# Tile 0's norm set before the memory's, routing weights stored four to a transfer, and the first head picked from the first block of scores

## The chip, the cores and the metric

One core of one Trainium2 chip runs the whole step in one launch. The metric is the device time in microseconds (us), the median of several runs. A core has five engines, each of which runs its own list of instructions in order: TensorE (PE, matrix products), VectorE (DVE), ScalarE (ACT), GpSimd (POOL) and SyncE (SP). Here SyncE issues all direct DMAs (loads, stores, spills), and GpSimd issues the gathers of experts.

## The reference, cut to what matters

One layer is computed for 1024 prompt tokens and 64 sample tokens. The mixer has three branches that share one input projection:

```
h = RMSNorm(x)                                  # gain g_attn
cols, gates = split(h @ w_in)
x = x + (sum_b sigmoid(gate_b) * (branch_b(cols) @ w_branch[b])) @ w_out
# branches: gated linear attention, forgetting attention, attention into 256 memory tokens
mem_k, mem_v = split(RMSNorm(mem) @ w_kv)       # mem_k gets a norm of its own, per head
```

The feed-forward part retrieves single-neuron experts:

```
h = RMSNorm(x)                                  # gain g_ffn
s[t, head, side, key] = (h @ w_q) . sub_keys    # 8 heads, 2 sides, 128 keys
top 16 of each side, top 16 of the 256 sums, softmax g
y = x + sum over heads and the 16: g * gelu(u[idx] . h) * v[idx]
```

All numbers are float32. Keys and values of both attentions, the forget gates and the linear attention's state are outputs too.

## The kernel before, in words

**Tiles and groups.** Tokens are cut into tiles of 128; tiles 0 to 7 are the prompt and tile 8 is the sample (64 tokens). Tiles go in groups: tile 0 alone, 1 and 2, 3 to 5, 6 to 8. For each group there are *front* steps (everything up to the scores), and for each tile, head and pair of experts an *expert* step ("pair").

**Front steps of a group** (`front_steps`, L141): `in_prep` norms a tile's tokens and transposes them (L1174, L1394, L826); `in_unit` multiplies one of 8 column chunks of `w_in` (1.8 MB each) with a tile (L839) and spills the result to `proj` (L560); `mix` and `fox` are the three branches for a tile, from columns loaded back (`load_P`, L574); `gate` (24 products), `out` (output projection, residual, second norm), and `sco`, four blocks of 512 score columns, that is two heads each, spilled to `sc_sp` (L719, L1094).

**Weights.** SyncE loads the weights of in, gate, out and sco steps as a sequence of items into two buffers in turn (`load_item`, L501): an item is issued when the item two before has been used. `next_item` (L528) is called ahead of the store of the same step. The score weights are not an input: `sub_keys` and `w_q` are multiplied once.

**The prologue** (`pre`, 23 steps e = 0 to 22, beside the front steps of tile 0). Step 0 loads and norms the memory (SyncE L752, ScalarE L1329, VectorE L1712, which wait for ten loads on one semaphore); steps 1 and 2 transpose it, 3 and 4 multiply it with `w_kv` (32 matmuls each), 5 transposes the keys. Steps 6 to 21 are the 16 routing products (L1141): block r of `w_q` (a wq buffer, one of three, loaded by `load_wq`) times block r of the sub-keys, into the PSUM tile `p_y`. ScalarE copies the even results (L1354) and VectorE the odd (L1740) to `rw[0]` and `rw[1]`; each waits for the store two before, because it writes the buffer that this store reads. SyncE stores each block to `rw_sp` (L783) in pieces of 512 bytes. TensorE waits at each step for the copy of the one before, as `p_y` is one tile.

**Experts.** `load_sc` (L727) loads a head's 256 scores; for the first head of a group it waits until all scores of the group are stored. `pick` finds the 16 best and their weights on VectorE in four pieces (L1699), the last of which lets GpSimd gather. A pair is two gathered rows of 8 KB per token: `gather` (L1768, three pairs ahead, ring of eight buffers), `dot` (L1663), `weigh` on ScalarE (L1311), product of the diagonal weights with the values on TensorE (L1151). For tiles of the first three groups VectorE takes the value of the second expert (`values`, L1675).

**The order** is written in a plan (`make_plan`, L157): a list of entries, each with one expert (or prologue) step and the front steps beside it. All 61 front steps of tile 0 come first, 23 of them with a prologue step, then `start` (pick of the first head, first gathers), then the 64 pairs of tile 0 with the front steps of tiles 1 and 2 beside them, spread by estimated weights over the first 48, and so on. Of an entry, SyncE and TensorE run the front steps first (`walk` with `front_first`), ScalarE and VectorE the expert step first (`trail`, L468); beside a pair these two also put off the copies of in, gate and sco steps until after the next pair's step. `in_prep` of a later group waits on SyncE until all scores of the group before are stored (L544), because tokens and scores share space.

```
    plan = [(None, [s]) for s, _ in front_steps(0)]
    for e in range(PRE_STEPS):
        at = e if e < 8 else e + 2
        plan[at] = (("pre", e), plan[at][1])
    plan.append((("start",), []))
```

## Time and profile before

| | us |
|---|---|
| median of three runs | 4381.66 |
| lowest and highest | 4379.17, 4395.21 |
| the profiled execution's own time | 4382.4 |
| its span, first to last instruction | 4380.7 |

| engine | busy us | share of the span |
|---|---|---|
| TensorE, matmul | 3387.2 | 77% |
| VectorE | 2805.3 | 64% |
| TensorE, weight load | 1760.2 | 40% |
| ScalarE | 1581.6 | 36% |
| GpSimd | 1218.1 | 28% |

The mean granted clock of TensorE is 0.881 of full speed. The DMA engines move 1471.58 MB, 336 GB/s over the span; the gathers take 65.7% of their time and the direct DMAs 20.5%. The chain that ended last is TensorE for 41%, DMA for 25%, VectorE for 18%.

How to read it: times are us unless marked ns. "c_ring" is the ring of gathered experts, which the prologue uses as its working space; "c_area" holds everything of the front steps; names with _sp are spills in HBM. In the rows below, "x16" counts instructions, and "[2.49 <-DMA rw_sp<-c_ring]" is the idle time of the engine before an instruction and what ended it, as inferred by the profile. In the chain of waits each row is what the next one waited for. A DMA's row in the chain runs from its issue to its landing. PEclk is the clock granted to TensorE, as a share of full speed.

### The profile page before, as it was taken

The page shows a single profiled execution, that of the slowest core. Times are in us where ns is not written, and L with a number is a line of the kernel's source. Part 1 is how long each engine was busy: PE and PEld are TensorE (multiplying, and loading weights), DVE is VectorE, ACT ScalarE, POOL GpSimd, SP SyncE. Part 2 cuts the span into 40 slices and gives each one's busy share as a digit, 9 for nine tenths or more (in the row PEclk, how much of TensorE's full clock was granted, in tenths as well). Part 3 has the DMA queues.
Part 4 walks back from the last instruction along what each step waited for, and adds up shares of the span by engine and source line. Part 5 has one row for each costly group of instructions (what it writes and reads, how often), then busy time and mean ns, then how long its engine had stood idle before and what let it go on. Part 6 is the DMA issues. An engine that isn't in the chain of part 4 may idle for free.

```text
span 4380.7 us, 33898 instructions
## 1 busy us (share of the span) xinstructions
PE 3387.2 (77%) x10219; PEld 1760.2 (40%) x10219; DVE 2805.3 (64%) x6049; ACT 1581.6 (36%) x3679; POOL 1218.1 (28%) x1122
## 2 busy tenths in 40 slices
PE   5785867985987778989599678567978777777766
PEld 2572445842434445544144344224533222222221
DVE  0213365557657785646877788676867777667687
ACT  1212154422226563432222465344433233333333
POOL 0001111213222222323333232242323344444433
PEclk9897978997997789999799778768999889999999
DMA  4767856889986787879999798888989999999998
GB/s 174 266 236 277 327 188 235 318 335 400 346 336 228 275 305 305 344 295 371 405 394 418 299 338 299 287 333 344 414 340 382 395 415 421 414 421 413 404 371 370
DMA packets 277901, 1471.58 MB, mean 336 GB/s; under 512 B 40581, under 2 KB 91781, under 8 KB 127125
## 3 DMA queue, kind: packets, MB, share of 16 engines
q0 software_dynamic: 156672, 1140.92, 65.7%
q1 hardware_dynamic: 121044, 328.49, 20.5%
q8 instruction: 81, 1.33, 0.1%
q14 instruction: 104, 0.84, 0.1%
HBM read 1408.90 MB, written 60.40 MB: 335 GB/s over the span
## 4 chain that ended last, share of the span: by engine, by line
PE 41%; DMA 25%; DVE 18%; issue 7%; ACT 6%; POOL 2%; SPq 1%; POOLq 0%; DVEq 0%; ACTq 0%
DMA c_ring<-in_uv,l_idx 17%; PE c_p_y L1154 11%; DVE c_ring L1670 7%; PE c_PB L850 4%; PE c_PC L850 4%; DVE l_ysb L1686 3%; PE c_PA L1107 3%; PE c_PA L1062 2%; PE c_PB L1062 2%; PE c_PC L1062 2%; PE c_PB L1107 2%; POOL c_ring L1784 2%; PE c_PA L1090 1%; PE c_PC L1065 1%; PE c_PB L1065 1%
## 5 line engine op out<-in xcount | busy, mean ns | idle before, releaser
L1784 POOL DMA_INDIRECT c_ring<-in_uv,l_idx x1088 | 1211.2, 1113 | 3139.1 <-PE c_p_y L1154 1341.4
L1154 PE MATMUL c_p_y<-c_ring,l_diag 128*128 128x512 f32 (+1 forms) x2816 | 1515.6, 678 | 443.3 <-ACT l_diag L1325 433.0
L1670 DVE CUSTOM_DVE_ANT_0 c_ring<-c_ring,l_h_cur 128x1024 f32<-128x1024 f32 x1088 | 1302.8, 1221 | 369.3 <-DMA c_ring<-in_uv,l_idx 360.7
L1154 PEld LDWEIGHTS c_p_y<-c_ring,l_diag 128*128 128x128 f32 (+1 forms) x2816 | 552.9, 207 | 1233.0 <-ACT l_diag L1325 643.6
L1317 ACT ACTIVATE l_gel<-l_dots 128x2 f32<-128x2 f32 x544 | 110.7, 203 | 1607.2 <-DVE l_dots L1670 1606.0
L1686 DVE SCALAR_TENSOR_TENSOR l_ysb<-c_ring,l_wgt,l_ysb 128x1024 f32<-128x1024 f32 x384 | 492.5, 1282 | 0.0
L1317 ACT ACT_TABLE_LOAD x207 | 265.6, 1283 | 59.8 <-DVE l_dots L1670 56.5
L1320 ACT ACTIVATE l_wgt<-l_gel,l_gw 128x1 f32<-128x1 f32 x1088 | 261.2, 287 | 17.9
L1325 ACT ACTIVATE l_diag<-c_ident,l_wgt 128x128 f32<-128x128 f32 x640 | 243.0, 399 | 16.7
L850 PE MATMUL c_PB<-c_area 128*128 128x451 f32 (+1 forms) x576 | 226.3, 545 | 0.0
L850 PE MATMUL c_PC<-c_area 128*128 128x451 f32 (+1 forms) x576 | 224.4, 541 | 0.1
L1062 PE MATMUL c_PA<-c_area 128*128 128x128 f32 (+3 forms) x512 | 132.3, 415 | 70.9 <-DMA c_area<-hT_sp 47.3
L850 PEld LDWEIGHTS c_PB<-c_area 128*128 128x128 f32 (+1 forms) x576 | 106.5, 186 | 117.4 <-issue 117.4
L850 PEld LDWEIGHTS c_PC<-c_area 128*128 128x128 f32 (+1 forms) x576 | 105.2, 183 | 117.4 <-issue 116.5
L1062 PEld LDWEIGHTS c_PA<-c_area 128*128 128x128 f32 x512 | 93.4, 203 | 110.6 <-issue 81.4
L1002 PE MATMUL c_PC<-c_ident,c_area 128*128 128x128 f32 (+2 forms) x328 | 66.3, 318 | 85.4 <-ACT c_area L1261 44.5
L1107 PE MATMUL c_PA<-c_area 128*128 128x512 f32 (+1 forms) x288 | 128.9, 601 | 1.9 <-ACT c_area L1283 1.9
L1107 PE MATMUL c_PB<-c_area 128*128 128x512 f32 (+1 forms) x288 | 127.9, 597 | 1.5 <-DMA c_area<-rw_sp 1.5
L1062 PE MATMUL c_PB<-c_area 128*128 128x128 f32 (+3 forms) x512 | 123.5, 395 | 0.0
L1062 PE MATMUL c_PC<-c_area 128*128 128x128 f32 (+3 forms) x512 | 122.9, 393 | 0.0
L1570 DVE TENSOR_TENSOR c_area<-c_area,c_PA 128x128 f32<-128x128 f32 (+3 forms) x32 | 14.0, 438 | 159.1 <-ACT c_area L1274 159.1
L1090 PE MATMUL c_PA<-c_area 128*128 128x512 f32 (+1 forms) x192 | 91.9, 636 | 21.2 <-DMA c_area<-in_w_out 18.1
(275 smaller groups left out, 3676.9 us busy)
## 6 DMA issues: line engine op xcount, KB each, us to landing
c_area<-in_w_gb SPq DMA_DIRECT2D x32, 2304.0 KB, 9.5
c_area<-in_w_in SPq DMA_DIRECT2D x32, 1804.0 KB, 9.4
c_area<-rw_sp SPq DMA_DIRECT2D x16, 2048.0 KB, 10.5
c_ring<-in_uv,l_idx POOLq DMA_INDIRECT x1088, 10.1
c_area<-in_w_out SPq DMA_DIRECT2D x8, 2048.0 KB, 9.7
proj<-c_area SPq DMA_DIRECT2D x64, 225.5 KB, 7.2
c_area<-proj SPq DMA_DIRECT2D x8, 1288.0 KB, 6.6
c_area<-in_x_all SPq DMA_DIRECT2D x16, 512.0 KB, 18.8
```

Source lines behind the costliest of these rows:

```text
L850: ins = mm_(banks[2 + u % 4][:T, :PW], hT_in[:, dt, j * 128:j * 128 + T], w[:, dt * PW:(dt + 1) * PW], start=dt == 0, stop=dt == DT - 1)
L1062: mm_(ps[:, 0:N], w[:, at:at + 128], g_hT[:, e, 0:N], start=e == 0, stop=e == DT - 1)
L1065: ins = mm_(ps[:, 512:512 + N], w[:, at:at + 128], g_oT[:, 4 * b + e, 0:N], start=e == 0, stop=e == 3)
L1090: ins = mm_((PA, PB)[j % 2][:T, half * 512:(half + 1) * 512], mixT[:, dt, j * 128:j * 128 + T], w[:, dt * 512:(dt + 1) * 512], start=dt == ...
L1107: ins = mm_(banks[v % 4][:T, :], hT_out[:, dt, j * 128:j * 128 + T], w[:, dt * 512:(dt + 1) * 512], start=dt == 0, stop=dt == DT - 1)
L1154: ins = mm_(p_y[:T, e * 512:(e + 1) * 512], diag[:, j, :T], ring[:, j, D + e * 512:D + (e + 1) * 512], start=r == 0 and q == 0 and k == 0, ...
L1317: a_(gel[:, c0:c0 + PAIR], dots[:, c0:c0 + PAIR], ACT.Gelu).then_inc(s_ae, 1)
L1320: ins = nc.scalar.mul(wgt[:, c0 + k:c0 + k + 1], gel[:, c0 + k:c0 + k + 1], gw[:, head % 3, c0 + k:c0 + k + 1])
L1325: ins = nc.scalar.mul(diag[:, (n * PAIR + k) % RING, :T], unit[:, :T], wgt[:, c0 + k:c0 + k + 1])
L1670: ins = nc.vector.tensor_tensor_reduce(out=ring[:, j, 0:D], in0=ring[:, j, 0:D], in1=h_cur[i % 2][:, :], scale=1.0, scalar=0.0, op0=ALU.mu ...
L1686: nc.vector.scalar_tensor_tensor(out=y[:T, :], in0=ring[:T, j, D:2 * D], scalar=wgt[:T, col:col + 1], in1=y[:T, :], op0=ALU.mult, op1=ALU. ...
L1784: nc.gpsimd.indirect_dma_start(out=ring[:, j, :], out_offset=None, in_=t_in["uv"][:, :], in_offset=bass.IndirectOffsetOnAxis(ap=idx[:, hea ...
```

## The change

There are three parts.

1. *The plan of the prologue.* Steps 0 to 7 move two entries down: the memory's norm stands beside unit 0 of tile 0, behind its norm, and its transposes beside units 1 and 2. Units 6 and 7, which stood alone, have steps 6 and 7 beside them. The loads of step 0 are a function of their own, `pre_loads`, which SyncE calls at the end of tile 0's first `in_prep`, at the same place in its list as before.
2. *Routing weights.* `rw` becomes two buffers of four blocks each. The copies go to a quarter of one (`rw_place`); only blocks 8 and later wait for a store. SyncE stores four blocks at a time, 2 MB in pieces of 16 KB a partition, at steps 10, 14, 18 and 22. The wq buffers lie elsewhere in the ring.
3. *Scores.* The last three `sco` steps of tile 0 leave the front. They stand first in the list beside tile 0's pairs: block 1 beside the first pair, blocks 2 and 3 beside the second; the two `in_prep` loads and norms of tiles 1 and 2 stand beside the third pair instead of the first. The later steps shift by up to two pairs: attention of tile 1 starts beside pair 13 instead of 11 (counted from 0), the first gate step stands beside pair 25 instead of 24, and from `out` steps on the two plans agree within a pair. `load_sc` waits for the store of its own block alone.

```diff
@@ -157,14 +157,15 @@
 def make_plan():
 
 
-    plan = [(None, [s]) for s, _ in front_steps(0)]
+    front = front_steps(0)
+    first, rest = front[:-3], front[-3:]
+    plan = [(None, [s]) for s, _ in first]
     for e in range(PRE_STEPS):
-        at = e if e < 8 else e + 2
-        plan[at] = (("pre", e), plan[at][1])
+        plan[e + 2] = (("pre", e), plan[e + 2][1])
     plan.append((("start",), []))
     for g in range(len(GROUPS)):
         pairs = [("pair", i, r, q) for i in GROUPS[g] for r in range(HEADS) for q in range(pairs_of(i))]
-        ahead = front_steps(g + 1) if g + 1 < len(GROUPS) else []
+        ahead = (rest if g == 0 else []) + (front_steps(g + 1) if g + 1 < len(GROUPS) else [])
         total = sum(w for _, w in ahead)
         slots = len(pairs) - 2 * pairs_of(GROUPS[g][-1])
         done, k = 0.0, 0
@@ -366,8 +367,11 @@
     m_ksq = rcube(2048, MT, BW)
     m_w = [rcube(8192 + n * 4096, DT, 512) for n in range(2)]
     skT = rcube(8192, 16, NK)
-    wq = [rflat[:, 10240 + k * 1024:11264 + k * 1024] for k in range(3)]
-    rw = [rcube(13312 + k * 1024, DT, NK) for k in range(2)]
+    wq = [rflat[:, at:at + 1024] for at in (14336, 15360, 5120)]
+    rw = [rcube(at, DT, 4 * NK) for at in (1024, 10240)]
+
+    def rw_place(r):
+        return rw[r // 4 % 2][:, :, r % 4 * NK:(r % 4 + 1) * NK]
     m_gk = sb("m_gk", [128, MD])
     m_st = sb("m_st", [128, MT, 4])
     kst = sb("kst", [128, MT, 3 * MH])
@@ -512,7 +516,7 @@
             elif kind == "sco":
                 if g == 0 and n == 0:
                     for r in range(2):
-                        sp.wait_ge(s_rw[r], 16 * HEADS)
+                        sp.wait_ge(s_rw[r], 32)
                 sp.dma_start(w[:, 0:4096], rw_sp[n]).then_inc(s_w[k % 2], 16)
             else:
                 sp.dma_start(w[:, 0:4096].rearrange("p (a b) -> p a b", a=DT),
@@ -536,6 +540,18 @@
 
         def load_x(t):
             sp.dma_start(xt[t % 2][:width_of(t), :], t_in["x_all"][rows(t), :]).then_inc(s_x[t % 2], 16)
+
+        def pre_loads():
+            sp.dma_start(m_x[:, :, :], t_in["mem"].rearrange("(a p) d -> p a d", p=128)).then_inc(s_pre, 16)
+            for n in range(2):
+                sp.dma_start(m_w[n][:, :, :], t_in["w_kv"][:, n * 512:(n + 1) * 512].rearrange(
+                    "(a p) n -> p a n", p=128)).then_inc(s_pkv, 16)
+            for dst, src, n in ((m_g[:, :], t_in["mem_g_in"], D), (m_gk[:, :], t_in["mem_g_k"], MD),
+                                (wa2[:, :], t_in["gla_w_a2"][0], None), (ba_bc[:, :], t_in["gla_b_a"], 256),
+                                (go_bc[:, :], t_in["gla_g_out"], GDV), (bf_bc[:, :], t_in["fox_b_f"], FH),
+                                (gq_bc[:, :], t_in["fox_g_q"], FD), (gk_bc[:, :], t_in["fox_g_k"], FD),
+                                (gm_bc[:, :], t_in["mem_g_q"], MD)):
+                sp.dma_start(dst, src if n is None else src[0:1, :].broadcast_to([128, n])).then_inc(s_pre, 16)
 
         def in_prep(g, p):
             t0, n = first_of(g), len(GROUPS[g])
@@ -549,6 +565,8 @@
                 if n > 1:
                     load_x(t0 + 1)
                 open_run(("in", g, 0))
+                if g == 0:
+                    pre_loads()
             elif p + 1 < n:
                 sp.wait_ge(s_h, t0 + p)
                 load_x(t0 + p + 1)
@@ -727,8 +745,8 @@
         def load_sc(n):
             i, r = ALL_HEADS[n]
             g = next(g for g in range(len(GROUPS)) if i in GROUPS[g])
-            if r == 0 and i == first_of(g):
-                scores_stored(g)
+            v = sco_unit(g, r // 2, i - first_of(g))
+            sp.wait_ge(s_cput[v % 3], 16 * (v // 3 + 1))
             sp.dma_start(sc[n % 2][:width_of(i), :], sc_sp[rows(i), r * 256:(r + 1) * 256]).then_inc(s_sc[n % 2], 16)
 
         def load_h(i):
@@ -750,17 +768,6 @@
             sp.dma_start(wq[r % 3][:, :], t_in["w_qT"][r * 128:(r + 1) * 128, :]).then_inc(s_wq[r % 3], 16)
 
         def pre(e):
-            if e == 0:
-                sp.dma_start(m_x[:, :, :], t_in["mem"].rearrange("(a p) d -> p a d", p=128)).then_inc(s_pre, 16)
-                for n in range(2):
-                    sp.dma_start(m_w[n][:, :, :], t_in["w_kv"][:, n * 512:(n + 1) * 512].rearrange(
-                        "(a p) n -> p a n", p=128)).then_inc(s_pkv, 16)
-                for dst, src, n in ((m_g[:, :], t_in["mem_g_in"], D), (m_gk[:, :], t_in["mem_g_k"], MD),
-                                    (wa2[:, :], t_in["gla_w_a2"][0], None), (ba_bc[:, :], t_in["gla_b_a"], 256),
-                                    (go_bc[:, :], t_in["gla_g_out"], GDV), (bf_bc[:, :], t_in["fox_b_f"], FH),
-                                    (gq_bc[:, :], t_in["fox_g_q"], FD), (gk_bc[:, :], t_in["fox_g_k"], FD),
-                                    (gm_bc[:, :], t_in["mem_g_q"], MD)):
-                    sp.dma_start(dst, src if n is None else src[0:1, :].broadcast_to([128, n])).then_inc(s_pre, 16)
             if e == 5:
                 sp.wait_ge(s_pp, 4)
                 sp.dma_start(skT[:, :, :], t_in["sub_kT"].rearrange("h c k -> c h k")).then_inc(s_psk, 16)
@@ -778,10 +785,10 @@
                 if r + 2 < 16:
                     sp.wait_ge(s_pp, e - 1)
                     load_wq(r + 2)
-                sp.wait_ge(s_pe, e - 1)
-                dst = rw_sp[(r - 1) // 4].rearrange("p (a b) -> p a b", a=DT)
-                sp.dma_start(dst[:, :, ((r - 1) % 4) * 128:((r - 1) % 4 + 1) * 128], rw[(r - 1) % 2][:, :, :])\
-                    .then_inc(s_rw[(r - 1) % 2], 16)
+                if r % 4 == 0:
+                    sp.wait_ge(s_pe, e - 1)
+                    n = r // 4 - 1
+                    sp.dma_start(rw_sp[n], rw[n % 2][:, :, :].rearrange("p a b -> p (a b)")).then_inc(s_rw[n % 2], 16)
 
         def start():
             load_sc(0)
@@ -1353,9 +1360,9 @@
             r = e - PRE_MEM - 1
             if r >= 0 and r % 2 == 0:
                 act.wait_ge(s_pp, e - 1)
-                if r >= 2:
-                    act.wait_ge(s_rw[0], 16 * (r // 2))
-                nc.scalar.copy(rw[0][:, :, :], h3(p_y[:, :], DT)).then_inc(s_pe, 1)
+                if r >= 8:
+                    act.wait_ge(s_rw[r // 4 % 2], 16)
+                nc.scalar.copy(rw_place(r), h3(p_y[:, :], DT)).then_inc(s_pe, 1)
 
         def start():
             soften(0)
@@ -1739,9 +1746,9 @@
             r = e - PRE_MEM - 1
             if r >= 0 and r % 2:
                 dve.wait_ge(s_pp, e - 1)
-                if r >= 2:
-                    dve.wait_ge(s_rw[1], 16 * (r // 2))
-                nc.vector.tensor_copy(rw[1][:, :, :], h3(p_y[:, :], DT)).then_inc(s_pe, 1)
+                if r >= 8:
+                    dve.wait_ge(s_rw[r // 4 % 2], 16)
+                nc.vector.tensor_copy(rw_place(r), h3(p_y[:, :], DT)).then_inc(s_pe, 1)
 
         def start():
             for piece in range(4):
```

## Rows read from the trace of the kernel before

**Rows 1.** Busy by stretch: length, PE, PEld, DVE, ACT, POOL, PEclk, DMA share, GB/s

```profile
408.20:416.50 8.30, 7.08 (x20) 4.68 (x21) 8.16 (x18) 4.05 (x7) 0.00 (x0) 0.50 0.76 311
416.50:542.00 125.50, 114.47 (x297) 55.91 (x295) 50.79 (x104) 21.11 (x57) 25.00 (x22) 0.98 0.87 327
542.00:726.00 184.00, 114.26 (x514) 80.15 (x514) 113.47 (x252) 100.11 (x199) 26.77 (x26) 0.74 0.58 209
726.00:880.00 154.00, 153.61 (x640) 123.00 (x641) 78.94 (x158) 62.02 (x113) 30.50 (x28) 0.98 0.77 291
```

**Rows 2.** Chain of waits, 20 to 60 us (start us, us, what)

```profile
31.09 8.81 DMA c_gm_bc<-in_mem_g_q
...
42.27 1.28 ACT L1337
...
44.16 1.28 DVE c_ring L1718
...
50.62 1.34 PE c_p_y L1118 x8
51.96 6.15 PE c_PB L850 x16
```

**Rows 3.** DMAs issued in 8 to 9.5 us (KB each, us to landing)

```profile
c_area<-in_x_all SPq DMA_DIRECT2D x1, 512.0 KB, 3.5
c_area<-in_g_attn SPq DMA_DIRECT2D x1, 512.0 KB, 5.2
```

**Rows 4.** Chain of waits, 98 to 160 us

```profile
104.70 0.64 DVE c_area L1416
...
106.76 10.62 DMA c_ring<-in_w_qT
...
117.52 3.76 PE c_p_y L1141 x16
121.28 7.07 PE c_PB L850 x16
...
143.35 1.95 DMA proj<-c_area
```

**Rows 5.** Timeline of TensorE, 78 to 260 us

```profile
152.80 0.38 PE L868 MATMUL c_PC<-c_ident,c_area 128*16 128x128 f32 x1 [6.24 <-DMA l_V<-proj]
...
195.60 3.78 PE L1141 MATMUL c_p_y<-c_ring 128*128 128x128 f32 x16 [3.65 <-DVE c_ring L1744]
```

**Rows 6.** Timeline of VectorE, 142 to 235 us

```profile
158.80 1.23 DVE L1744 COPY c_ring<-c_p_y 128x1024 f32<-128x1024 f32 x1 [2.49 <-DMA rw_sp<-c_ring]
```

**Rows 7.** Timeline of ScalarE, 142 to 235 us

```profile
206.23 1.01 ACT L1358 COPY c_ring<-c_p_y 128x1024 f32<-128x1024 f32 x1 [9.66 <-DMA rw_sp<-c_ring]
...
221.40 1.01 ACT L1358 COPY c_ring<-c_p_y 128x1024 f32<-128x1024 f32 x1 [1.51 <-DMA rw_sp<-c_ring]
```

**Rows 8.** DMA issued at 194.8 us (KB each, us to landing)

```profile
c_ring<-in_w_qT SPq DMA_DIRECT2D x1, 512.0 KB, 9.8
```

**Rows 9.** Chain of waits, 314 to 420 us

```profile
338.61 15.46 PE c_PA L1107 x32
...
362.74 7.15 PE c_PB L1107 x16
...
370.62 7.88 DMA sc_sp<-c_area
378.52 2.30 DMA l_sc<-sc_sp
...
390.71 1.12 POOL c_ring L1784
...
403.51 0.40 ACT l_diag L1325
```

**Rows 10.** DMA issued at 347.8 us (KB each, us to landing)

```profile
sc_sp<-c_area SPq DMA_DIRECT2D x1, 256.0 KB, 8.2
```

**Rows 11.** Timeline of TensorE, 405 to 500 us

```profile
428.74 1.88 PE L1154 MATMUL c_p_y<-c_ring,l_diag 128*128 128x512 f32 x4
```

## The prediction

> **What bounds the kernel now.** I read four views: busy time by stretch, the chain of waits, the timelines of single engines, and the DMA issues with their time to landing. The change touches the first 420 us and, through the moved score steps, the pairs of tile 0, which last until about 1078 us; nothing later changes but its start. Each engine runs a list in fixed order, so a shift at the start is carried to the end.
>
> Stretches [rows 1]: after 416.5 TensorE is busy 114.5 of 125.5 us at a granted clock of 0.98 (projection units of tiles 1 and 2); from 542 to 726 it is busy 114 of 184 us at 0.74, a latency-bound stretch of attention steps; from 726 to 880 it is full (153.6 of 154). So in two of three stretches a microsecond of TensorE work is a microsecond of time. Ahead of them the chain is serial: loads, a few instructions, one product.
>
> The start [rows 2]: the last of the memory's small loads lands at 39.9, ScalarE and VectorE norm the memory, and only behind that tile 0. TensorE gets the memory's transposes at 50.6, though tile 0's own input is there early: its tokens were issued at 7.8 and landed 3.5 us later, the gain, issued at 8.2, 5.2 us later [rows 3]. The chain then runs through the projection units, the key load, the last unit and its store [rows 4], through tile 0's attention steps with the routing products between [rows 5 to 8], and through scores, store, load, pick and first gather [rows 9].
>
> **Part 1, the norm's place.** Tile 0's norm needs tokens and gain (13.4), then square and root (2.5 with a table load), multiply 1.3, transposes 2.0, copy 1.0: about 20. Units 0 and 1 (6.15 each, at half clock at first) end by 35, beside loads that must land anyway, so they cost nothing. Late weights have 9 us of slack, since TensorE next waits for the memory until 44.2. That is 39.9, two squares 2.3, two roots 0.3 to 0.6, then the multiply of 1.28; the table load of 1.28 in the chain [rows 2] falls out, as tile 0's root has loaded that table.
>
> From 50.6 to 104.7 TensorE did, without a gap, two sets of memory transposes, four units and two memory products. The changed plan puts the same list behind 44.2 (units 2 to 5 in place of 0 to 3): 6.4 sooner. But it idled for 9 us before. After idle time rows show half speed: 3.76 us for 16 matmuls, the unit behind it 7.07 instead of 6.15 [rows 4]. That takes some 2 back: 4.5 sooner. Unit 2's weights queue behind the preloads and land about 46; if 2 us late, so is everything.
>
> Those 4.5 us move the sub-key and wq loads, issued at the end of that list: the first routing product starts at 112.9 instead of 117.4. Behind it stood unit 4, a product, a wait for the next weights, and units 5 to 7, to 142.7. Now only unit 7 is left: 112.9 + 3.76 + 7.07 = 123.7, copy 0.64, store 1.95: projections stored at 126.4 instead of 145.3, **19 sooner**. Their reload took until 152.8 [rows 5]. In its way now stand the memory-key store and one wq load (1 MB), issued a microsecond earlier. 2 MB ahead of a score store makes it land 8.2 us after issue [rows 10] against 1.95 for a store alone [rows 4], so 1 MB is up to 3; I take 2 (they start to drain a microsecond before). **-17.**
>
> Beside the rule: the Trainium skill, ScalarE: Activation LUTs, section What ACT_TABLE_LOAD costs, puts a switch of table at about 2.66 us, a drain of 1.38 behind the load. From the start of the load here to VectorE's multiply, with a root between, 1.89 us pass (42.27 to 44.16), which leaves no room for it, so the trace disagrees; by the page's figure part 1 would give 1.4 us more.
>
> **Part 2, four routing blocks to a store.** Sixteen stores of 512 KB become four of 2 MB, and copies no longer wait for the store two before. Three such waits are on the chain. VectorE's copy at 158.8 sat idle 2.49 us [rows 6]; its product, begun behind the matmul at 152.8 [rows 5] at half speed (3.7 us), was done at 156.7: -2.1. ScalarE's copy at 206.2 stood idle 9.66 us [rows 7] while its product (3.78 us from 195.6) was done at 199.4 [rows 5]; but the next product needs a wq block issued at 194.8 that lands 9.8 later, at 204.6 [rows 8], behind the gate weights. So 207.3 becomes 204.6: -2.7, not -7. The one at 221.4 idled 1.51 us [rows 7], which bounds it; its product comes just ahead, so -0.4. **-5.2** together. The 2 MB stores ahead of wq loads cost nothing as long as these have slack; the last, issued near 223 of the old clock, has drained when the gate loads start at 233: zero, at worst 2.
>
> Start of the scores: -17 - 5 = **-22** (bounds -17 and -25).
>
> **Part 3, the first head from the first block.** In the old clock: score block 0 ends at 347.0, its store is issued at 347.8 and lands at 356.0 [rows 10], the score load takes 2.3. The pick, which began at 380.8, begins at 358.3: 22.5 sooner; so are the first gather (390.7 to 368.2) and the first weights (403.9 to 381.4) [rows 9]. But three score blocks of 7.15 are still owed. Block 1 fills TensorE's wait (to 354.1). Blocks 2 and 3 stand on its list behind the first pair's product: 381.4 + 3.6 (half clock) + 7.15 + 7.15 + 2 (clock) = about 401.5.
>
> Then comes the wait that replaces the old one. SyncE stores block 3 at 402.3, behind a load of projection weights that it may issue only when block 3 is done. The same pair of transfers now takes 7.88 [rows 9]: 410.2. Only then may it load tiles 1 and 2, whose input shares space with the scores; the first tokens land 3.5 later, gain and second tile by 417. Square, root, multiply: transposes at about 418 instead of 408.2. **+10.** Queued behind that wait on SyncE is only the plan's own next step; ScalarE and VectorE stall in the norm with pair 3 behind them, TensorE with pair 2.
>
> To set against it: two pairs are done before the norm that used to follow it. Counting the plan, units are still beside 11 pairs, but attention steps are beside 12 instead of 13 and gate steps beside 13 instead of 14. The second is worth a pair's 1.7 to 1.9 us of TensorE [rows 11] (full there), the first between 1.7 and 8 (a pair takes 14 us of that stretch, part of it cover): 4. **+10 - 6 = +4** (bounds -4 and +10).
>
> **Sum: -22 + 4 = -18.** The profiled execution took 4382.4 (span 4380.7, 1.7 around it), so 4364.4; the median shown is 0.7 below it, so **4364 us**, -0.4%. A measurement here can tell about 0.5%, 22 us, from no change.
>
> The Trainium skill, TensorE: Matmul & The Clock Gate, What's actually happening, says that the throttled clock is the default and that activity releases it. The trace agrees (0.50 granted from 408.2 to 416.5 after 38 us idle [rows 1]); it speaks against part 3, which cuts one idle stretch into two, each with its slow beginning; in the sum this stands by the rows.
>
> **The rivals.**
> *Hidden score steps (0.35).* The two idle stretches take the moved blocks as a whole and the attention stretch gives back 8 us, or tokens land sooner: part 3 is -4 to 0, total -22 to -28, about 4357. For it: TensorE idles from 369.9 to 408.2, 38 us [rows 1, 9]. Against: the norm waits for block 3's store.
> *Longer wait for tile 1 (0.10).* Gathers share the DMA with block 3's store and the tokens, and no pair is given back: part 3 is +12, total -10: 4372.
> *Loads rule the start (0.04).* Unit weights land late each time, so part 1 keeps only the 6 us of the earlier memory norm: total -6 to -8, 4375.
> *Slower (0.04).* The 2 MB stores sit on SyncE's queue ahead of wq blocks and gate weights. One costs up to 8.2 - 1.95 = 6.3 us for what is behind it. It decides only where the block behind has less slack; were all four on the path, +25 on my -18: 4389. Against: the products' loads run one step ahead.
> That the change does not do what it says has no chance of note: every list is written out.
>
> **How the numbers follow.** My forecast, -12 to -22, has 0.47. Faster by over 0.5% is the first rival, 0.35; slower the last, and only a part of it passes half a per cent: 0.03; the rest 0.62. The range takes in most of the first two rivals: 4350 to 4379.
>
> **What would show it.** Tile 0's transposes near 16 us and the memory's at 44; proj reload issued at 126; no idle time ended by rw_sp; first score matmul at 316.6; first gather 45 us sooner, near 346; tile 1's transposes near 396, only 12 sooner; the first pair of tile 1 18 sooner. I am wrong if wq landings end waits of products before 200, if tile 1's transposes move by 20 or more, or if the lead at the scores is not the lead at 726.

## The result and the profile after

| | before | after |
|---|---|---|
| median, measured side by side (20 runs each), us | 4389.76 | 4376.84 |
| lowest and highest, us | 4379.15, 4399.85 | 4370.53, 4387.11 |
| ratio after to before | | 0.9974 [0.9964, 0.9983] |
| profiled span, us | 4380.7 | 4372.0 |

The change makes the kernel 0.26% faster, 11.4 us of 4381.66, where the prediction said 18. It is less than the half per cent that a single comparison of this kernel can tell, but with 20 runs on each side the interval lies clear of 1, and just clear of the forecast's 0.9960 (4364 over 4381.66). The kernel before was profiled in one of its quicker executions (4382.4 us, its median here is 4389.76), so a difference between two profiles at their ends comes out some 7 us smaller than the medians have it.

The page of the changed kernel, sections 1, 2 and 4:

```profile
PE 3394.4 (78%) x10219; PEld 1765.7 (40%) x10219; DVE 2803.7 (64%) x6049; ACT 1576.0 (36%) x3675; POOL 1219.8 (28%) x1122
...
DMA packets 261835, 1471.57 MB, mean 337 GB/s; under 512 B 40388, under 2 KB 75204, under 8 KB 110548
...
PE 42%; DMA 25%; DVE 18%; issue 6%; ACT 6%; POOL 2%; SPq 1%; POOLq 0%; DVEq 0%; ACTq 0%
```

Busy times and shares are those of before within 0.4%. What changed is small against the span and lies in its first tenth, so the page can't explain it; the chain and the timelines can. There are fewer packets (277901 before), and all that are gone belong to the direct transfers, from the wider routing stores.

**The start.** TensorE's timeline, 10 to 60 us, after:

```profile
15.86 1.97 PE L843 MATMUL c_PA<-c_ident,c_area 128*128 128x128 f32 x8 [15.86 <-DVE c_area L1413]
...
44.78 1.97 PE L1125 MATMUL c_p_y<-c_ident,c_ring 128*128 128x128 f32 x8 [11.76 <-DVE c_ring L1725]
```

Tile 0's transposes now stand at 15.86, the memory's at 44.78 instead of 50.6 [rows 2]. The chain of waits, 98 to 160 us, after; it answers rows 4:

```profile
102.94 10.49 DMA c_ring<-in_w_qT
...
117.32 6.43 PE c_PC L857 x16
...
124.43 1.99 DMA proj<-c_area
...
127.46 7.45 DMA l_V<-proj
```

One unit instead of four stands behind the key load, so the last projection store begins at 124.43 instead of 143.35 [rows 4], 18.9 us sooner. TensorE's timeline, 130 to 232 us, after; it answers rows 5:

```profile
134.95 0.38 PE L875 MATMUL c_PC<-c_ident,c_area 128*16 128x128 f32 x1 [6.05 <-DMA l_V<-proj]
...
185.69 3.75 PE L1148 MATMUL c_p_y<-c_ring 128*128 128x128 f32 x16 [4.17 <-DMA c_ring<-in_w_qT]
...
200.79 2.02 PE L1148 MATMUL c_p_y<-c_ring 128*128 128x128 f32 x16 [0.96 <-DMA c_ring<-in_w_qT]
```

Attention of tile 0 begins 17.9 us sooner than in rows 5. Behind it no engine is released by a store to `rw_sp` any more; in place of the waits of rows 6 and 7 stand two waits of TensorE for the block of `w_q` itself, 5.1 us together. The block of the first is issued right behind the gate weights (175.94 us), that of the second 2.1 us behind a 2 MB store of routing weights (192.85 and 190.74).

**The scores and tile 1.** The chain of waits, 314 to 420 us, after; it answers rows 9:

```profile
315.76 8.86 PE c_PA L1114 x16
...
325.26 8.30 DMA sc_sp<-c_area
...
345.79 1.12 POOL c_ring L1791
...
358.68 3.78 PE c_p_y L1161 x4
362.46 14.40 PE c_PB L1114 x32
...
377.66 14.86 DMA sc_sp<-c_area
392.53 3.73 DMA c_area<-in_x_all
...
397.44 1.28 ACT L1189
398.74 0.30 ACT l_stat L1189
...
400.67 1.98 PE c_PA L843 x8
```

The scores begin 22.8 us sooner than in rows 9, the first gather 44.9 us sooner. But the store of score block 3, issued at 377.66, takes 14.86 us to land where the same store took 7.88 [rows 9], and the tokens of tile 1 wait for it. At the transposes of tile 1 the lead of 22.8 has shrunk to 7.6 (400.7 against the 408.2 of rows 1). **Part 3 took back 15.2 us of 22.8.**

Busy by stretch, after: the last four rows answer rows 1, the first three cut up the idle time that used to be one piece (columns as in rows 1).

```profile
324.50:362.46 37.96, 10.76 (x22) 4.52 (x21) 17.47 (x61) 5.24 (x12) 8.98 (x8) 0.66 0.79 304
362.46:376.94 14.48, 14.48 (x33) 6.36 (x33) 7.76 (x21) 3.73 (x10) 1.87 (x2) 0.96 0.98 387
376.94:400.70 23.76, 1.65 (x5) 0.41 (x3) 2.21 (x4) 4.06 (x7) 1.87 (x2) 0.58 0.79 312
400.70:408.50 7.80, 6.61 (x20) 4.50 (x21) 7.64 (x13) 3.64 (x5) 0.00 (x0) 0.53 0.05 19
408.50:536.30 127.80, 114.38 (x297) 55.86 (x295) 48.14 (x94) 18.48 (x56) 23.26 (x22) 0.97 0.87 323
536.30:723.80 187.50, 118.73 (x511) 85.31 (x511) 111.21 (x253) 99.37 (x197) 24.84 (x24) 0.68 0.54 193
723.80:874.60 150.80, 149.37 (x628) 121.04 (x628) 71.08 (x142) 55.68 (x100) 27.49 (x26) 0.98 0.75 287
```

TensorE is idle for 27.2 us of the first row and for 22 of the third, 49 in all; before, the one idle stretch ahead of tile 1 was 38. Behind the transposes the stretches of units and attention are longer than before, so that the full one begins at 723.8, its fellow of before at 726.4: of the 7.6 us only 2.6 are left there.

### The profile page after: what moved, and what is told of

Read it like the earlier page. It is cut to its first block, busy times and chain, and to the rows that moved or that the text cites. A ratio compares the mean times of both kernels' runs of the same rounds, so it can differ in the third digit from the quotient of the medians.

```text
span 4372.0 us, 33943 instructions
## 1 busy us (share of the span) xinstructions
PE 3394.4 (78%) x10219; PEld 1765.7 (40%) x10219; DVE 2803.7 (64%) x6049; ACT 1576.0 (36%) x3675; POOL 1219.8 (28%) x1122
## 4 chain that ended last, share of the span: by engine, by line
PE 42%; DMA 25%; DVE 18%; issue 6%; ACT 6%; POOL 2%; SPq 1%; POOLq 0%; DVEq 0%; ACTq 0%
DMA c_ring<-in_uv,l_idx 18%; PE c_p_y L1161 11%; DVE c_ring L1677 6%; PE c_PB L857 4%; PE c_PC L857 4%; DVE l_ysb L1693 3%; PE c_PA L1114 2%; PE c_PA L1069 2%; PE c_PB L1069 2%; PE c_PB L1114 2%; PE c_PC L1069 2%; POOL c_ring L1791 2%; PE c_PA L1097 1%; DMA c_area<-in_w_out 1%; DMA l_V<-proj 1%
## 5 line engine op out<-in xcount | busy, mean ns | idle before, releaser
L1327 ACT ACTIVATE l_wgt<-l_gel,l_gw 128x1 f32<-128x1 f32 x1088 | 261.2, 287 | 17.9
L1332 ACT ACTIVATE l_diag<-c_ident,l_wgt 128x128 f32<-128x128 f32 x640 | 243.1, 399 | 16.7
## 6 DMA issues: line engine op xcount, KB each, us to landing
c_area<-in_w_out SPq DMA_DIRECT2D x8, 2048.0 KB, 10.1
```

The source lines that it names most:

```text
L1327: ins = nc.scalar.mul(wgt[:, c0 + k:c0 + k + 1], gel[:, c0 + k:c0 + k + 1], gw[:, head % 3, c0 + k:c0 + k + 1])
L1332: ins = nc.scalar.mul(diag[:, (n * PAIR + k) % RING, :T], unit[:, :T], wgt[:, c0 + k:c0 + k + 1])
```

## The experiments

Sixteen runs, each timed in five rounds beside the kernel before (4 to 12 executions each); e10 and e16 are the changed kernel again, e11 is e4 and e12 is e8. The first table gives the ratios, the second the profile: by how many us the first matmul of a stage starts sooner (-) or later than in the kernel before. The transposes of tile 1 stand at 408.2 there, the first score step of tiles 1 and 2 at 928.8.

| run | part of the change | median us | ratio, 95% interval |
|---|---|---|---|
| e1 | 1 alone | 4374.00 | 0.9960 [0.9944, 0.9977] |
| e2 | 2 alone | 4383.56 | 0.9992 [0.9979, 1.0005] |
| e3 | 3 alone | 4404.82 | 1.0031 [1.0019, 1.0044] |
| e4 | 1 and 2 | 4359.35 | 0.9929 [0.9910, 0.9948] |
| e11 | 1 and 2 again | 4368.25 | 0.9939 [0.9918, 0.9959] |
| e10, e16 | all three again | 4379.02, 4379.28 | 0.9968 [0.9954, 0.9981], 0.9977 [0.9963, 0.9991] |
| e5 | all, weights behind tokens | 4372.78 | 0.9945 [0.9928, 0.9962] |
| e6 | all, score steps beside pair 0 | 4367.23 | 0.9925 [0.9907, 0.9943] |
| e7 | e5 and e6 | 4364.23 | 0.9919 [0.9901, 0.9937] |
| e8 | e7, tokens at the start | 4353.29 | 0.9896 [0.9875, 0.9917] |
| e12 | e8 again | 4355.25 | 0.9912 [0.9888, 0.9936] |
| e9 | e8, weights early | 4347.36 | 0.9900 [0.9878, 0.9922] |
| e13 | all, head 2's load later | 4375.56 | 0.9964 [0.9949, 0.9979] |
| e14 | all, store before weights | 4373.69 | 0.9967 [0.9953, 0.9981] |
| e15 | e13 and e14 | 4372.73 | 0.9965 [0.9947, 0.9982] |

| run | scores of tile 0 | transposes of tile 1 | scores of tiles 1, 2 | end of the profile |
|---|---|---|---|---|
| changed | -22.8 | -7.6 | -4.5 | -8.6 |
| e1 | -16.4 | -16.5 | -12.6 | -8.3 |
| e2 | -1.6 | -1.2 | -1.1 | -0.6 |
| e3 | +0.3 | +15.8 | +19.3 | +15.2 |
| e4, e11 | -23.0, -22.6 | -21.9, -22.2 | -22.2, -18.3 | -15.2, -14.5 |
| e10, e16 | -23.7, -22.1 | -7.3, -6.5 | -5.4, -4.8 | -4.0, +3.6 |
| e5 | -23.1 | -16.6 | -18.3 | -23.5 |
| e6 | -23.0 | -20.1 | -16.9 | -11.2 |
| e7 | -24.7 | -30.4 | -31.3 | -37.3 |
| e8, e12 | -22.9, -22.9 | -44.8, -45.1 | -31.9, -32.9 | -28.5, -25.1 |
| e9 | -23.3 | -41.8 | -40.7 | -39.5 |
| e13, e14 | -22.2, -23.0 | -10.6, -10.1 | -7.7, -9.1 | -2.1, -7.6 |
| e15 | -25.8 | -12.2 | -8.9 | -14.2 |

How far to trust a row: each stands for one profile. The changed kernel stands three times in the table. Up to the transposes of tile 1 its profiles agree within 1.6 us, at the end they spread over 12. The fourteen profiles that have parts 1 and 2 run the same steps as far as the scores, and these start between 312.8 and 316.5 us, so a difference of one profile to another below some 3 us says little. At the end the rows show some 8 us less gain than the ratios in the mean, as the kernel before was profiled in a quick execution. So steps are judged at the transposes and the whole by the ratios.

### Each part alone, and the change without part 3

e1 takes the edits of part 1 alone:

```diff
     for e in range(PRE_STEPS):
-        at = e if e < 8 else e + 2
-        plan[at] = (("pre", e), plan[at][1])
+        plan[e + 2] = (("pre", e), plan[e + 2][1])
```

with `pre_loads` as in the change. e2 has `rw_place`, the places of `rw` and `wq`, the stores of four blocks and the copies' waits. e3 has these:

```diff
-    plan = [(None, [s]) for s, _ in front_steps(0)]
+    front = front_steps(0)
+    first, rest = front[:-3], front[-3:]
+    plan = [(None, [s]) for s, _ in first]
...
-            if r == 0 and i == first_of(g):
-                scores_stored(g)
+            v = sco_unit(g, r // 2, i - first_of(g))
+            sp.wait_ge(s_cput[v % 3], 16 * (v // 3 + 1))
```

and `ahead` with `rest` for tile 0. e4 is the changed kernel with these undone.

> Part 1 alone (the prologue's steps two entries down) on the kernel before. Theory 1 (part 3 is the term that was mis-sized; the lead of the start is kept to the end): first scores 17 to 18 us sooner, end 17 us sooner, ratio about 0.996. Theory 2 (a lead gained at the start is partly eaten beside the pairs of tile 0, whatever made it): first scores 17 sooner, end 8 to 10 sooner, ratio about 0.998.

> Part 2 alone (four routing blocks to a store). Both theories: first scores 5 us sooner, with the waits for rw_sp gone. Theory 1: end 5 us sooner, ratio 0.9988. Theory 2: end 2 to 3 sooner, ratio 0.9994. The rival that the 2 MB stores hold up wq blocks and gate weights would show as an end later than before, 1.001 or more.

> Part 3 alone (first head from the first block, three blocks beside the first pairs). Theory 1: first gather 22 us sooner, but block 3's store lands some 15 us after issue and tile 1's transposes come 12 to 15 us later than before; end 8 to 12 us later, ratio 1.002 to 1.003. Theory 2: end no more than 4 us later, ratio 1.000 to 1.001.

> The changed kernel with part 3 undone (parts 1 and 2 stay). Theory 1: tile 1's transposes and the end both 22 us sooner than before, ratio 0.995, which is some 10 us under the changed kernel. Theory 2: transposes 22 sooner, end 10 to 13 sooner, ratio 0.997, the same as the changed kernel.

Part 1 alone moves the scores by 16.4 us, and its attention of tile 0 starts 17.3 sooner. By its ratio (0.9960) the lead is kept to the end, as the first theory has it; the end of its profile (-8.3) fits the second, but that column is the weak one. Part 1 keeps the waits for the routing stores. Its chain of waits, 120 to 240 us:

```profile
179.66 11.21 DMA rw_sp<-c_ring
...
200.23 5.57 DMA rw_sp<-c_ring
```

Part 2 alone takes these away and gains 1.6 us, less than a third of the 5.2 forecast. Its chain of waits, 150 to 225 us:

```profile
194.12 9.26 DMA c_ring<-in_w_qT
...
210.67 9.62 DMA c_ring<-in_w_qT
```

The wait for the store is gone and the wait for the next block of `w_q`, some 9 us from issue to landing, has its place: twice, where the prediction counted it once. The first of these loads stands behind the gate weights. The second, issued at 210.67, stands behind a 2 MB store of routing weights issued at 208.56, and TensorE sits idle 2.76 us for it (0.96 in the changed kernel). On top of part 1 the same edit is worth 6.6 us (23.0 against 16.4). So parts 1 and 2 together give what was forecast, -22, and the second is worth four times as much behind the first. Part of that is the shorter second wait; with one profile of each the rest stays open.

Part 3 alone costs 15.8 us at the transposes and has a ratio above 1; undone, it gives the changed kernel 14.3 us there (21.9 against 7.6). The chains of waits show the store of block 3, in e3:

```profile
401.09 14.78 DMA sc_sp<-c_area
```

and in e4, followed by the load of the first head:

```profile
349.36 7.78 DMA sc_sp<-c_area
357.16 2.29 DMA l_sc<-sc_sp
```

In the changed kernel and in e3 it lands after 14.8 to 14.9 us; with all four blocks in the front, after 7.8 as in rows 9.

### What makes the store late: the weights ahead of it

SyncE issues ahead of block 3's store two loads of projection weights, 1.8 MB each. e5 holds both back behind the tokens of tiles 1 and 2:

```diff
-            if j == len(GROUPS[g]) - 1:
+            if j == len(GROUPS[g]) - 1 and not (g == 0 and k >= 2):
                 next_item(("sco", g, k))
...
                 open_run(("in", g, 0))
+                if g == 1:
+                    next_item(("sco", 0, 2))
+                    next_item(("sco", 0, 3))
```

e6 gives the three moved score steps no weight in the plan, so that all three stand beside the first pair and the later steps stay beside the pairs that they had before:

```diff
-    first, rest = front[:-3], front[-3:]
+    first, rest = front[:-3], [(s, 0.0) for s, _ in front[-3:]]
```

e7 has both edits.

> The changed kernel, with the two loads of projection weights of tiles 1 and 2 held back on SyncE until behind the loads of their tokens. Theory A (block 3's store landed after 14.9 us because 3.6 MB of weights stood ahead of it on SyncE's queue): the store lands 4 to 6 us after issue, tile 1's transposes 8 to 11 us sooner than in the changed kernel (near 391), end 8 to 10 sooner, ratio 0.995. Theory B (the gathers of tile 0's pairs share the DMA and set that time): the landing stays above 10 us, transposes move by less than 4, ratio 0.997.

> The changed kernel with the three moved score blocks at no weight in the plan, so that all three stand beside the first pair and everything from the norm of tiles 1 and 2 on stands beside the pairs of the kernel before. Theory A1 (the credit for pairs done sooner is false: the shifted plan itself costs time from the transposes to the gate steps): that stretch, 323 us in the changed kernel, is 318 to 319 again as before, and the transposes come near 386 since blocks 2 and 3 fill the idle time; end some 18 us sooner than the changed kernel, ratio 0.993. Theory B1 (the stretch is 323 because of the lead, not of the plan): it stays at 322 to 324.

> Both edits, score blocks beside the first pair and weights behind the tokens. Block 3's copy near 360, its store landed by 366, tokens by 371: transposes near 376, 24 us sooner than in the changed kernel and 10 sooner than with part 3 undone; end 30 us under the kernel before, ratio 0.991 to 0.993. If gathers set the time, transposes near 386 and a ratio near that of part 3 undone (0.993).

The chain of waits of e5, 372 to 400 us:

```profile
377.70 2.25 DMA sc_sp<-c_area
379.97 7.29 DMA c_area<-in_x_all
...
391.68 1.98 PE c_PA L846 x8
```

With the weights gone the store lands in 2.25 us instead of 14.86. The tokens pay back a part: 7.29 instead of 3.73, with the gathers beside them. Transposes 9.0 sooner than in the changed kernel, ratio 0.9945 against 0.9974. So the two loads on SyncE's queue made this store late.

It doesn't follow that gathers leave a store alone. When block 3's store is issued the first burst of gathers is over: in e5 its 2.25 us pass with no gather in them. The DMA view of e5, 377.5 to 380 us:

```profile
q1 hardware_dynamic: 144, 0.26, 27.6%
```

q1 is SyncE's queue and its 0.26 MB are the store; q0, the gathers' queue, has no row. In the changed kernel nothing of a gather moves from 377 to 381 us either, and from the issue of the store to its landing 3.44 MB go over q1 and 2.10 over q0. Twelve us earlier it is otherwise. The DMA view of e5, 365 to 373 us, when block 1's store is under way with nothing else on SyncE's queue:

```profile
q0 software_dynamic: 429, 3.12, 93.3%
q1 hardware_dynamic: 144, 0.26, 8.5%
...
sc_sp<-c_area SPq DMA_DIRECT2D x1, 256.0 KB, 7.5
```

The same 256 KB take 7.5 us beside the gathers alone.

The chain of waits of e6, 355 to 392 us:

```profile
361.41 18.69 DMA sc_sp<-c_area
380.12 3.51 DMA c_area<-in_x_all
```

The store is issued 16.3 us sooner and is the slowest of all, 18.69: the three stores and both weights loads are issued within 2 us, and at that time gathers fill the DMA (1.02 MB of theirs and nothing else from 359.5 to 362 us). The transposes still gain 12.6. e7 has the same three stores at the same point and no weights ahead. Its chain, 350 to 382 us:

```profile
359.05 10.79 DMA sc_sp<-c_area
```

So some 8 of the 18.7 us are the weights; of the rest the gathers have the larger part, as one store alone beside them takes 7.5. The transposes of e7 are at 377.9, 22.8 before the changed kernel's.

On the credit, e6 decides nothing. From the transposes of tile 1 to the first gate step it takes 320.5 us; kernels with the old plan take 316.2 to 322.2, those with the shifted plan 318.4 to 323.6, and the two theories were 3 to 6 us apart.

### Is it the load directly ahead, or SyncE that was held?

Between the stores of blocks 1 and 2 SyncE stood from 365.9 to 373.2 us in the score load of head 2, whose new wait is for block 1's store, the one that takes 7.6 us beside the gathers. So the two weights loads were issued at 373.6 and 376.9, 3.3 us apart; in e4 they are 8.8 apart. e13 moves that score load from pair 0 to pair 3, where all scores are long stored; e14 issues block 3's store ahead of the second weights load; e15 does both; e16 is the changed kernel on the same chip.

```diff
         def pair(i, r, q):
             n = i * HEADS + r
+            if n == 0 and q == 3:
+                sp.wait_ge(s_sfree, 1)
+                load_sc(2)
             if q == 0:
...
-                if n + 2 < len(ALL_HEADS):
+                if n and n + 2 < len(ALL_HEADS):
```

```diff
-            if j == len(GROUPS[g]) - 1:
+            late = g == 0 and k == 3
+            if j == len(GROUPS[g]) - 1 and not late:
                 next_item(("sco", g, k))
...
+            if late:
+                next_item(("sco", g, k))
```

> The changed kernel, with the load of head 2's scores issued at pair 3 instead of pair 0, so that SyncE isn't held at 365.9 to 373.2 us by the wait for block 1's store. Cause 1 (SyncE held): the first weights load and block 2's store are issued near 370 instead of 373.6, the second weights load stays at 376.9 (it waits for block 3's matmuls), block 3's store has 3 to 4 us less in front of it: it lands in 10 to 12 us instead of 14.9, tile 1's transposes near 397 instead of 400.7, ratio 0.996. Cause 2 (the load directly ahead): the store lands in 14 to 15 us as before, transposes within 1 us of 400.7, ratio 0.997.

> The changed kernel, with block 3's store issued ahead of the second weights load instead of behind it. Cause 2: the store has only the rest of the first weights load in front of it, issued 4 us before: it lands in 5 to 9 us instead of 14.9; the tokens, now behind the second weights load, take 6 to 9 instead of 3.7; together transposes at 394 to 398, ratio 0.995 to 0.996. Cause 1: the first weights load and block 2's store, issued late, are what fills the queue: the store still needs 11 us or more, and with the slower tokens nothing is gained (transposes 399 to 402).

> Both edits. If each takes away its part: block 3's store lands in 2.3 to 4 us, tokens in 7 to 9, transposes at 389 to 393, near the 391.7 of the kernel with both weights loads held back, ratio 0.9945. If only one of the causes is at work, it stands within 1.5 us of the better of the other two runs.

> The changed kernel beside them on the same chip: ratio 0.997, transposes of tile 1 at 400.7 to 400.9, block 3's store 14.5 to 15 us.

The chains of waits from the store to the tokens, e13:

```profile
378.12 11.43 DMA sc_sp<-c_area
389.56 3.63 DMA c_area<-in_x_all
```

e14:

```profile
376.98 6.61 DMA sc_sp<-c_area
383.61 10.11 DMA c_area<-in_x_all
```

e15:

```profile
376.66 4.14 DMA sc_sp<-c_area
380.81 10.84 DMA c_area<-in_x_all
```

In e16 the two take 15.4 and 3.5 us. Both causes are real for the store: 4.0 us come from SyncE being held, 8.8 from the load directly ahead. But what e14 takes from the store it gives to the tokens, which now stand behind the same 1.8 MB. From the issue of the store to the landing of the tokens it is 18.9 us in e16, 15.1 in e13, 16.7 in e14 and 15.0 in e15, against 9.6 in e5, where nothing big stands ahead of either. The held SyncE is worth 3.8 us alone and 1.7 with the swap; the swap is worth 2.2 alone and 0.1 on top. The ratios (0.9964 to 0.9967 against 0.9977 on that chip) point the same way, but their intervals overlap. Two of the expectations missed: the tokens behind a weights load take 10.1 to 10.8 us instead of 6 to 9, and so e15 has its transposes at 396.1, not at 389 to 393, and e14 at the late end of its 394 to 398 (398.1).

### Can the early pick be had without its price?

In e7 tile 1's norm still waits for block 3's store, because tokens and scores share space. e8 moves the three score buffers up by 512 columns, out of the tokens' space, and loads the tokens at `start`. In its new place a score buffer shares space with the outputs of the units, so the copies of tile 1's first units wait for the scores' stores; the first norm waits for the last score product:

```diff
-    sco = [flat(A0 + 7680 + k * 512, 512) for k in range(3)]
+    sco = [flat(A0 + 8192 + k * 512, 512) for k in range(3)]
...
         def start():
...
             load_x1(0)
+            tokens(1)
...
+                if g == 1 and p == 0:
+                    act.wait_ge(s_cmm, 4)
...
+                if g == 1 and k == 0:
+                    for q in range(3):
+                        act.wait_ge(s_cput[q], 16 * every(4, 3, q))
```

`tokens(1)` is what `in_prep` issued: both tiles and the gain. e9 takes the two weights loads out of `in_prep` and issues them at score block 1, ahead of that block's store and of head 2's load:

```diff
+            if g == 0 and k == 1:
+                next_item(("sco", 0, 2))
+                next_item(("sco", 0, 3))
             sp.wait_ge(s_cev[v % 2], v // 2 + 1)
             sp.dma_start(sc_sp[rows(t), k * 512:(k + 1) * 512], sco[v % 3][:T, :]).then_inc(s_cput[v % 3], 16)
```

> As before, and the tokens of tiles 1 and 2 are loaded at the start of the pairs, ahead of any wait for a store of scores (the score buffers move by 512 columns so that they overlap only the projections' spill, whose first copies wait). If the store of block 3 is all that holds tile 1's norm, the transposes come right behind the first pair's step on VectorE, near 366, and the end is another 8 to 10 us sooner than with both edits: ratio 0.989 to 0.991. If the weights' landing takes its place, units of tile 1 start no sooner than with both edits and the ratio is the same.

> The kernel with both changes and the tokens loaded at the start (4353.3 us, ratio 0.990 to before), and beside it the weights of tile 1's in unit, 2 MB, issued at score block 1 instead of behind the stores. In it the weights landed at 377.1 us and set the first matmul of tile 1's in unit, while tile 1's transposes had been done from 363.4. Theory A, the weights' place on SyncE's queue sets it: they land before the picked rows of the later pairs are wanted, the in unit begins near 366 to 371, and the step of 6 to 11 us is kept as far as tile 1's gate unit (ratio 0.987 to 0.989). Rival B, the queue is only moved: the 2 MB now lie in front of the gathers of the first pairs and of the stores of picked rows, the first pair starts later by the 3 to 8 us that such a load takes, and nothing is gained (ratio 0.990 to 0.992).

> The kernel with both changes (score steps all beside the first pair, weights' loads behind the tokens) and tile 1's tokens loaded at the start, once more beside the changed kernel: ratio 0.989 to 0.991, which is 25 to 30 us under the changed kernel, if the earlier result holds; within 10 us of it if that was a difference of the chip.

> The changed kernel once more, to stand beside the next two on one chip. Both theories: 11 to 13 us under before (ratio 0.997).

> The changed kernel with part 3, the early pick, undone, once more. If the early pick costs time in this kernel, this one is below the changed kernel by some 10 to 20 us on the same chip (ratio 0.992 to 0.994 against 0.997); if the pick is neutral and the difference between the earlier runs was one of the chip, both stand within 4 us of each other.

In e8 the transposes of tile 1 are at 363.4, 44.8 us before the old ones. The chain of waits of e8, 355 to 380 us, shows what is late next:

```profile
361.48 15.62 DMA c_area<-in_w_in
377.15 3.37 PE c_PB L865 x4
```

The first unit begins 13.8 us behind the first transpose, released by its weights, and of the 44.8 only 31.9 reach the next scores. e9 issues them sooner, and its chain, 340 to 380 us, has them off the path:

```profile
346.82 11.04 DMA c_ring<-in_uv,l_idx
...
374.42 5.69 PE c_PB L865 x15
```

Now the first gather lands 11.04 us after issue (7.5 in e12) and the transposes are 3 us later. The units start at 374.4 instead of 377.0: sooner, but not the 366 to 371 that the theory of the queue's place asked for. Both theories are half right: the place on the queue was the limit, and what takes it shares the DMA with the gathers. By the profile e9 leads e12 by 7.8 us at the next scores and its median is 7.9 lower, but the intervals of the ratios overlap. e8, e9 and e12 beat both kernels clearly: about 1% under before and 0.6 to 0.8% under the changed kernel.

Side by side on one chip the change without part 3 (e11) is 10.8 us below the changed kernel (e10) by the medians, and 14.8 sooner at the transposes; the first pair of such runs gave 14.3 at the transposes. So the early pick, as written, costs 11 to 15 us. The intervals of e10 and e11 just overlap; those of the changed kernel and e4 do not.

## Why the prediction was right or wrong

**Part 1 (-17): right.** Measured -17.9 with the change and -17.3 alone. Memory transposes at 44.78 (44.2 worked out), projection stores landed at 126.42 (126.4), attention at 134.95. The 126.4 is luck in part: the first routing product came 0.7 later than the 112.9 worked out and the unit behind it was 0.6 shorter than the 7.07. From that landing to attention it took 8.5 us, 1.0 more than before, where 2 were booked.

**Part 2 (-5.2): right in the sum, wrong as an edit of its own.** With part 1, -23.0 - (-16.4) = -6.6. Alone, -1.6: a block of `w_q` lands 9 us after its issue twice, not once, the second time behind a 2 MB store, which the prediction had set at zero.

**Start of the scores (-22): right**, -22.8.

**Part 3 (+4): this is the step that failed**, by the size of two of its terms. It came out at +15.2 in the changed kernel, +15.5 alone (15.8 - 0.3).

1. *"The same pair of transfers now takes 7.88 [rows 9]: 410.2."* It took 14.86, 7.0 us more. The rows of before showed the store behind one load of 1.8 MB, issued a microsecond ahead; e4, which has the same order, shows that the load before it had landed by then (347.1 us, the store is issued at 349.4). In the new order SyncE is held by head 2's load, so two loads and block 2's store stand close together ahead of it: 3.6 MB, of which the last part drains beside gathers. The prediction listed what is queued behind the norm's wait, but not what is queued behind the *other* wait that the change adds, the one in `load_sc`; and that wait is long because block 1's store now runs beside the first gathers (7.6 us). e5, e13 and e14 show both.
2. *"+10 - 6"*: the credit for two pairs done earlier isn't there. The pairs moved exactly as counted: by the products of tile 0's pairs, the attention stretch has 12 beside it instead of 13 and the gate stretch 13 instead of 14. But from tile 1's transposes to the scores of tiles 1 and 2, eight profiles with the shifted plan (changed, e3, e5, e10, e13 to e16) take 518.8 to 524.2 us, 522.6 in the mean, and seven with the old one (before, e1, e2, e4, e6, e7, e11) 519.6 to 524.5, 522.0 in the mean (e8, e9 and e12, whose tokens come early, are left out). The credit measures 0 within a spread of 6, where 6 were booked. That zero is a sum of parts: with the shifted plan the units of tiles 1 and 2 take 1.9 us longer (134.8 to 136.5 against 132.6 to 134.1), attention 0.6 and the gate steps 0.5, and the output steps are 2.4 shorter (49.6 to 49.8 against 51.6 to 53.5). The first and the last of these are clear of the spread; no run tells why.
3. The other way: a slow beginning of 2 us was booked for blocks 2 and 3. They took 14.40 for 32 matmuls, full speed; only the pair's product ahead of them was slow, 3.78, which was booked too. Together with scores that were 0.8 sooner, block 3's store was issued 2.6 us before the 380.3 worked out.

The account closes at the transposes of tile 1: +10 + 7.0 for the store, -1.8 for the blocks, +0.2 for the tokens, with nothing for the credit, is +15.4 against 15.2. That leaves 7.6 us of the start's 22.8, where the ratio makes 11.4 of the whole kernel (7.4 to 15.8 by its interval); which of the two is nearer the rest of the kernel the runs can't tell.

Why the attention and gate steps give nothing back is read from the profile, not tested. TensorE's waits in the attention stretch, 536 to 723.7 us, after:

```profile
PE c_PC L1009 <- ACT c_area L1268: 28.2, 12, 7.6
PE c_PC L875 <- DMA l_V<-proj: 13.4, 1, 13.4
```

The same view of before has 23.4 and 11.4 us. The stretch goes from wait to wait (ScalarE's exponentials, a reload, and at its end the reload of the normed tokens). With a pair less beside it these waits are longer, which fits a pair that ran inside them. In the chain of waits, 640 to 726 us, the last of them is, after (14.01 us before):

```profile
707.99 15.71 DMA c_area<-hT_sp
```

The gate stretch has a pair less and TensorE is busy 149.37 us of it instead of 150.6, and the stretch is still 150.8 long.

**The clock.** It was granted at 0.66 over the first idle stretch with its product, rose to 0.96 over the blocks, and was 0.53 when the transposes of tile 1 came (the 0.50 of rows 1). That is a second slow beginning, as booked. The Trainium skill, TensorE: Matmul & The Clock Gate, What's actually happening, says that the clock is throttled unless activity releases it. The trace agrees; the price of the slow beginning at the first pair is 1.9 us for one product of four matmuls (3.78 against 1.88) and no more.

**The rule on the table load** stays refuted: the load of 1.28 us at 397.44 has its root begin at 398.74, 0.02 behind its end. The Trainium skill, ScalarE: Activation LUTs, What ACT_TABLE_LOAD costs, has another 1.38 there; no run here shows it on the path.

**The rivals.** What came is nearest to the second one, "Longer wait for tile 1", given 0.10: its sum was -10, and the measured ratio makes -11.4; that no pair is given back is what the profiles show. The cause that it named for the store is not the one that was found: it had the gathers, and e5, e13 and e14 show SyncE's own loads, with the gathers behind the hold of SyncE. The first, given 0.35 (part 3 at -4 to 0), is refuted by e3 and e4. Of "Slower" a small part came: one 2 MB store stands ahead of a block of `w_q` that TensorE waits 0.96 us for. The loads of units didn't rule the start. The forecast's own band, -12 to -22, ends just short of the result; the range, 4350 to 4379, holds it.

**The signs.** The start came as written: transposes at 15.86, first score product at 315.76 (316.6 worked out), first gather at 345.79, nothing ended by `rw_sp`. Of the signs of being wrong, one was met outright: the 22.8 us at the scores are 2.6 at the gate steps, near 726. A `w_q` landing ends a wait at 185.69, before 200, but the forecast's own sum holds that wait (204.6 in the old clock, less 17 or so), so this sign was badly placed. The products at the start of tile 1's pairs come 4 to 5 us sooner (1090.6 to 1086.4, 1103.4 to 1098.4), not 18.

## What to carry to other kernels

When a store lets a later load go, its price is set by what was issued on its queue in the microseconds ahead of it and by what other queues move meanwhile, so redraw both for the new order instead of taking the landing time from the old trace; and every wait that an edit adds to the issuing engine bunches what comes behind it. Changing the order of two transfers that both stand ahead of the work mostly moves the wait from one to the other (2.2 us were left of 8.8 here); putting the large one behind both took 9 us, and taking the dependence away (other space, an earlier load) took the store off the path. Work taken out from beside stretches that wait on other engines gave nothing back here, and of two edits that remove waits in the same place the second was worth several times what it was worth alone.

## What was not expected of the hardware

A store of 256 KB on SyncE's queue landed after 2.25 us with nothing large ahead of it and no gather moving (e5, 377.7 us), and after 7.5 us with nothing ahead of it and gathers at 93% of the DMA time (e5, 365.8; 7.6 in the changed kernel). It took 7.8 behind one load of 1.8 MB without gathers (e4), 11.4 with two loads 7 us apart (e13), 14.8 to 15.9 with two loads some 3 us apart (changed, e3, e10, e16), 10.8 behind two stores of its own size beside full gathers (e7), and 18.7 with both loads and the three stores issued within 2 us beside full gathers (e6). So the burst of the first gathers costs so small a store about as much as a load of 1.8 MB ahead of it on its own queue. Tokens of 512 KB took 3.5 to 3.7 us behind a drained queue with next to no gather moving but 7.3 with the gathers beside them (e5).

The Trainium skill, DMA: Bandwidth & Descriptors, Queues, rings and completion order, says that within one queue descriptors are consumed in order and that an engine takes turns between queues. The rows agree with the first part: the store waits for what its own queue holds. Of the turns they show only that they are no shield for a small transfer, 7.5 us against 2.25; how the turns are shared out no run isolates.

The granted clock can come back within one product: after 27.2 us without a matmul, four matmuls took 3.78 us at half speed and the 32 behind them 14.40 at full speed.
